# The first block products of a gMLP and MLP layer, taken row tile by row tile, with two sums moved to GpSimd

## What is computed

```python
def trunk(x):                                   # x: 1024 x 1024
    hn = rms_norm(x, norm1_g)
    u, v = split(gelu(hn @ a_w_in), 2)          # a_w_in: 1024 x 4096
    v = layer_norm(v) * a_ln_g
    sv = causal(a_ws) @ v + a_bs                # by chunks of 128 positions, 8 groups
    x = x + (u * sv) @ a_w_out                  # 2048 x 1024
    x = x + square(relu(rms_norm(x, norm2_g) @ mlp_w1)) @ mlp_w2
    return rms_norm(x, final_g)
```

## Time and profile before

| | us |
|---|---|
| median of 3 runs (1134.77 to 1135.09) | 1135.06 |
| the profiled execution, its own time | 1135.68 |
| its span in the trace | 1133.9 |
| PE busy | 1121.9 |
| DVE busy | 770.3 |
| ACT busy | 568.1 |
| POOL busy | 35.1 |

### The profile page before, as it was taken

One profiled execution on the slowest core, in us unless ns is written; L12 is line 12 of the kernel. 1 busy time (PEld: TensorE's weight loads), 2 busy tenths in 40 slices (PEclk: granted clock), 3 DMA queues, 4 the chain that ended last, 5 costly groups with the idle time before them and its releaser, 6 DMA issues.

```text
span 1133.9 us, 13195 instructions
## 1 busy us (share of the span) xinstructions
PE 1121.9 (99%) x5155; PEld 934.3 (82%) x5155; DVE 770.3 (68%) x832; ACT 568.1 (50%) x868; POOL 35.1 (3%) x22
## 2 busy tenths in 40 slices
PE   9999999999999999999999999999999999999997
PEld 8788888888888888888888888888888888888886
DVE  6986655578668986657667547456589575677666
ACT  8663434543554334656664464554653343433446
POOL 4000000000000000000000000000000000000240
PEclk9999999999999999999999999999999999999999
DMA  9054253262866494431343534527788254343213
GB/s 334 1 186 149 75 181 117 75 227 109 306 225 248 135 349 158 155 103 46 103 164 142 193 141 154 191 101 273 295 302 316 97 237 186 108 152 112 77 73 148
DMA packets 74765, 191.17 MB, mean 169 GB/s; under 512 B 3120, under 2 KB 4176, under 8 KB 68048
## 3 DMA queue, kind: packets, MB, share of 16 engines
q1 hardware_dynamic: 74496, 190.07, 46.4%
q10 hardware_dynamic: 208, 0.28, 0.1%
HBM read 131.61 MB, written 58.72 MB: 168 GB/s over the span
## 4 chain that ended last, share of the span: by engine, by line
PE 93%; ACT 2%; DVE 2%; issue 1%; DMA 1%; SPq 0%; DVEq 0%; ACTq 0%
PE banks L397 30%; PE banks L401 30%; PE banks L402 30%; PE banks L466 2%; DVE left_and_right L1289 1%; DMA rows<-in_x_dram 1%; PE banks L504 0%; ACT junk_b L1185 0%; ACT ring_high L894 0%; DVE ring_low L1253 0%; DVE raw_s L1358 0%; DVE rows L1433 0%; DVE scratch L1418 0%; ACT rows L1220 0%; ACT a_high L951 0%
## 5 line engine op out<-in xcount | busy, mean ns | idle before, releaser
L924 ACT ACTIVATE pair_high<-left_and_right 128x1024 fp32r<-128x1024 f32 x168 | 177.7, 1061 | 255.8 <-PE banks L397 208.1
L1253 DVE TENSOR_TENSOR ring_low<-left_and_right,ring_high 128x512 fp32r<-128x512 f32 x224 | 153.0, 691 | 213.1 <-ACT ring_high L894 212.7
L1261 DVE TENSOR_TENSOR pair_low<-left_and_right,pair_high 128x1024 fp32r<-128x1024 f32 x168 | 204.6, 1229 | 123.2 <-ACT pair_high L924 123.1
L894 ACT ACTIVATE ring_high<-left_and_right 128x512 fp32r<-128x512 f32 x224 | 139.4, 631 | 272.9 <-PE banks L397 175.9
L397 PE MATMUL banks<-pair_high 128*128 128x512 f32 x672 | 262.0, 390 | 0.1
L402 PE MATMUL banks<-pair_high,pair_low 128*128 128x512 f32 x672 | 261.5, 389 | 0.0
L401 PE MATMUL banks<-pair_low,pair_high 128*128 128x512 f32 x672 | 261.4, 389 | 0.0
L397 PE MATMUL banks<-s_high,ring_high 128*128 128x512 f32 x384 | 149.6, 389 | 0.0
L401 PE MATMUL banks<-s_low,ring_high 128*128 128x512 f32 x384 | 149.4, 389 | 0.0
L402 PE MATMUL banks<-s_high,ring_low 128*128 128x512 f32 x384 | 149.4, 389 | 0.0
L397 PEld LDWEIGHTS banks<-pair_high 128*128 128x128 f32 x672 | 126.1, 188 | 26.9 <-issue 0.4
(11 more groups left out here) (105 smaller groups left out, 1227.7 us busy)
## 6 DMA issues: line engine op xcount, KB each, us to landing
left_and_right<-sums SPq DMA_DIRECT2D x40, 1024.0 KB, 6.1
left_and_right<-in_mlp_w_dram SPq DMA_DIRECT2D x36, 1024.0 KB, 6.3
sums<-rows SPq DMA_DIRECT2D x34, 1024.0 KB, 5.1
left_and_right<-in_a_w_in_dram SPq DMA_DIRECT2D x19, 1024.0 KB, 6.2
v_blocks<-rows SPq DMA_DIRECT2D x8, 1024.0 KB, 4.5
left_and_right<-in_a_w_out_dram SPq DMA_DIRECT2D x8, 1024.0 KB, 10.3
spare<-v_blocks SPq DMA_DIRECT2D x6, 1024.0 KB, 5.8
sums<-spare SPq DMA_DIRECT2D x6, 1024.0 KB, 3.9
```

Source lines behind the costliest of these rows:

```text
L894: nc.scalar.activation(ring_high[k][:, :], right_place(n, pos)[:, k, :], ACT.Copy)\
L924: nc.scalar.activation(pair_high[pair_entry(d, pos, k)][:, :, :], pair_of(d, pos, k), ACT.Copy)\
L1253: nc.vector.tensor_tensor(ring_low[k][:, :], right_place(n, pos)[:, k, :], ring_high[k][:, :].bitcast(F32), ALU.subtract).then_inc(low_don ...
L1261: nc.vector.tensor_tensor(pair_low[e][:, :, :], pair_of(d, pos, k), pair_high[e][:, :, :].bitcast(F32), ALU.subtract).then_inc(low_done, 1)
```

## The change

1. The first product (A11) runs row tile by row tile. `first_turn(c)` turns the four k-tiles of row tile c into the one bank 4 + c, and `first_products(c, k)` makes the four units' share of that row tile. Row tiles 2 and 3, and A12, are turned between these products. The high and low part of A11 are now taken per row tile, and all ring places stay in use until row tile 3.
2. The gain is no longer per partition there, so DVE multiplies it in with the tile's scale: a row of `norm1_g` is loaded, spread over the partitions by a matmul with a row of ones (bank 3), and copied to `g1_b`.
3. A12's high and low part come straight from the banks. A21 and A22 are turned inside the second product by halves of 8 transposes, through the two banks 6 and 7.
4. S3 is made from the banks by k-tiles (`first_s3`, high part of A11 minus the gained A21) and completed by one sum with A11's low part (`first_s3_rest`); S2 and its split go by k-tiles. S4 takes two sums in place of one.
5. `raw_a11` isn't copied; POOL makes it again as high + low (`restore_a11`). The first weight sum moves from DVE to POOL (`first_sum_t`). Both stand ahead of the masking of `ws_nat` in POOL's list.
6. SP loads row tile 0, the first weight k-tile, row tile 1, the rest of that weight block, and then the other row tiles.

```diff
-            def first_turn():
-
+            def first_turn(c):
+
+                bank = 4 + c
+                begin_fill(("turn", 0, "a11"), bank)
+                pe.wait_ge(x_scaled, c + 1)
                 for k in range(4):
-                    begin_fill(("turn", 0, "a11"), 4 + k)
...
+            def first_block():
+
+                first_turn(0)
+                warm(FILL_A)
+                first_turn(1)
+                warm(FILL_B)
                 for c in range(4):
-                    pe.wait_ge(x_scaled, c + 1)
+                    first_products(c, 0)
+                    if c == 3:
+                        turn_half("a12", 1)
+                    first_products(c, 1)
+                    if c == 1:
+                        first_turn(2)
+                    if c == 2:
+                        turn_half("a12", 0)
+                    first_products(c, 2)
+                    first_products(c, 3)
+                    if c == 1:
+                        first_turn(3)
...
+            def next_block():
+
+                for m in range(4):
                     for k in range(4):
...
+                        next_products(m, k)
+                        if (m, k) in NEXT_TURNS:
+                            turn_half(*NEXT_TURNS[m, k])
...
             pe.wait_ge(ident_done, 1)
-            warm(3 * WARM_UP)
+            warm(2 * WARM_UP)
+            pe.wait_ge(g_row_landed, 16)
+            pe.wait_ge(ones_set, 1)
+            begin_fill("g_row", 3)
+            nc.tensor.matmul(ps[:, 3, :], one_row[:, :], g1_row, start=True, stop=True).then_inc(full[3], 1)
+            warm(2)
...
+            load_x(0)
             sp.dma_start(quarter[0][:, 0:1, :], weight(0, "b11")[:, 0:1, :]).then_inc(first_landed, 16)
+            load_x(1)
             load(("b11", 0), quarter[0][:, 1:4, :], weight(0, "b11")[:, 1:4, :], quarter_landed[0], "quarter0")
...
+            def first_s3(k):
...
+                nc.vector.scalar_tensor_tensor(out=raw_s3[:, k, :], in0=ps[:, bank, :], scalar=minus_g1[:, k:k + 1],
+                                               in1=high["a11"][:, k, :].bitcast(F32), op0=ALU.mult, op1=ALU.add)\
+                  .then_inc(drained[bank], 1)
...
                 if n == 0:
-                    low_combo(0, "a12")
-                    sum_t(0, 0)
-                    split_low(0, 1, 0)
-                    split_low(0, 1, 1)
-                    sum_combo(0, "s3")
-                    split_low(0, 1, 2)
-                    sum_combo(0, "s2")
-                    split_low(0, 1, 3)
+                    for k in range(4):
+                        first_s3(k)
+                    first_s3_rest()
+                    sum_t(0, 1)
+                    for k in range(4):
+                        first_s2(k)
...
+            def restore_a11():
+
+                for c in range(4):
+                    emptied(pool, ("turn", 0, "a11"), 4 + c)
+                nc.gpsimd.tensor_tensor(raw_a11[:, :, :], high["a11"][:, :, :].bitcast(F32),
+                                        low["a11"][:, :, :].bitcast(F32), ALU.add).then_inc(a11_restored, 1)
+
+            def first_sum_t():
+
+                q = {b: quarter[i][:, :, :] for b, i in places(0).items()}
+                pool.wait_ge(*landed["b12", 0])
+                pool.wait_ge(low_done, unit(0, 0, 3) + 1)
+                nc.gpsimd.tensor_tensor(q["b11"], q["b12"], q["b11"], ALU.subtract).then_inc(t_summed, 1)
...
             for m in range(MT - 2):
                 scale_x_b(m)
+            first_sum_t()
+            restore_a11()
             pool.wait_ge(ws_landed, 16)
```

385 lines of the change are left out of this document (262 added, 123 removed).

## The result

| | before | after |
|---|---|---|
| median, us | 1134.91 (5 runs, 1134.76 to 1135.09) | 1147.91 (5 runs, 1145.19 to 1149.40) |
| ratio, 95% interval | | 1.0112 [1.0102, 1.0123] |
| profiled execution, us | 1135.68 | 1149.40 |
| its span, us | 1133.9 | 1147.7 |
| S2's start, us | 43.24 | 56.98 |

What follows compares the result with a forecast made beforehand. PE bounds the kernel, but DVE decides S2's start: -1.1 (early start) + 3.5 + 3.3 (POOL holds) - 0.4 (turn waits) = +5.3 us on 1135.68, so 1141.0 profiled, 1140.4 as median; range 1132.5 to 1143.0.

Steps and rivals of the forecast that it cites:

- the landmark: Start of S2's product, the third, 43.24 us before: what it gains or loses, the whole kernel gains or loses.
- The start, 11.2: Kernel start: the first product matmul begins near 11.2 us, 2.6 us earlier than before.
- eight warm-ups: PE between the first two turns: 16 instructions, each like a transpose or slightly more, take 1.8 us.
- The holds, 3.5 and 3.3: DVE ahead of S2: POOL's two sums, 4.0 us each, hold `ring_low` 0 for 3.5 and the next `ring_low` for 3.3.
- PE's turn waits vanish in that (-0.4): DVE ahead of S2: its two waits for PE's half turns, 0.5 us, mostly disappear within the holds, saving 0.4.
- The 17.0 of the forecast: DVE's own instructions from `ring_low` 0 of the second product to S2, summed to 16.9 or 17.0 us.
- The sign for PE's last release: At S2's product, starting at 48.6: PE is released by `ring_low` and not by `s_low`.
- Case B: Ahead of S2: one POOL sum is hidden, about 0.9 us of its hold left; 1138.0 us, chance 0.18.
- Case C: Ahead of S2: POOL's sums cost nothing, leaving -1.1 us; 1134.0 us, chance 0.26.
- The gain of 1.1 us: At S2's start: new landmark 42.1 against 43.24, as long as POOL disturbs nobody.
- Case D: At S2: PE, not DVE, decides if DVE's list begins before 21 us; 1131.0 at best, 1132.5 for half, chance 0.16.
- the dear end of A: Ahead of S2: both POOL sums hold DVE, 1140.4 us, chance 0.40; with holds of 5.2 us each, 1142.8.

Runs made afterwards that it cites:

- e3: Changed kernel with the first T (weight) sum moved back to DVE, POOL keeping only the restoring of A11: 1147.44 us.
- e5: Changed kernel with each of POOL's two sums in four instructions of 512 elements in place of one of 2048: 1140.00 us, ratio 1.0041.
- e1: Changed kernel with both POOL sums (first weight sum, restoring of A11) given to DVE: 1141.99 us, ratio 1.0057.
- e9: e1 with sixteen identity products ahead of S2's product, one output block lost: 1141.52 us, in two groups, 1137.3 to 1137.8 and 1141.5 to 1141.8.
- e7: Changed kernel with 14 and 20 identity products behind the first two steps of the second product: 1150.21 us.
- e2: Changed kernel with the restoring of A11 moved back to DVE, POOL keeping only the first T (weight) sum: 1145.16 us.
- e10: Changed kernel's row-by-row start without POOL sums, weight sums and S2 in pieces, S1 as A21 + A22, late mask, part of output lost: 1136.40 us, ratio 1.0009.
- two small edits: Kernel before with POOL's mask waiting for the sixth product and S2's low part in four instructions, PE waiting for each k-tile: 1132.66 us, ratio 0.9981.
- e11: Kernel before with one wait added, so that POOL's mask of ws_nat waits for the sixth product's ring: 1134.36 us, ratio 0.9994.
- e4: Changed kernel with 16 warm-up identity products in place of 8 ahead of the spreading of the gain row: 1147.77 us.
- e6: Changed kernel with the gain row spread by a DMA in place of matmul and copy, and twelve warm-up products: 1147.10 us.
- e8: Kernel before with only the first T (weight) sum moved from DVE to POOL, ahead of the mask: 1137.08 us, ratio 1.0015.

## Why the prediction was right and wrong

The direction and the mechanism were right: DVE, not PE, bounds the stretch ahead of S2, POOL's two sums hold it, and the landmark carries the whole difference. The time was not: 1147.9 against a range up to 1143.0. The forecast put S2's start at 48.6; it is at 56.98, 8.4 us later. By its own steps:

- **The start, 11.2.** Measured 14.54 in the profiled execution. The order of the chain held, and the price of the spreading nearly (2.07 us against 1.7). The step that failed is PE's rate at the start, above all in "eight warm-ups (16 instructions, each like a transpose or slightly more, 1.8)". They took 3.37, which is 1.4 us of the miss by the distance to the next turn; 1.6 us more were lost ahead of row tile 0's turn, which began at 10.12 and not near 8.5, behind six identity instructions in 1.65 us that take 0.94 in e3. The rate was read from a kernel whose clock was up at 5.7 us, and this one's came up at 13.9. In other executions (e3, e5) 11.2 came true. Cost: 3.3 us, all of it handed on, since DVE's list began at 27.39, 3.3 us after the forecast's 24.1.
- **The holds, 3.5 and 3.3.** Measured 3.8 (4.52 less 0.69) and 5.1 (5.97 less the usual 0.9). The mis-sized term is the price of one POOL sum, taken as 4.0 "nearer the lower end": it is 4.55 and 4.97. The second sum met no `ring_low` but a scaling, which took 4.7 us, a hold of 4.3. The other 0.8 belong to a term that the forecast put at nothing: POOL's mask, now queued behind the sums, held the second scaling (1.3 in place of 0.5, the mask running from 36.24 for 1.28), as it did in e1. The forecast had read that hold in the kernel before, and counted it as gone without a reason. Cost: 0.3, 1.0 and 0.8, together 2.1 us. The figure that the prediction quoted beside it, 4497 ns for one POOL sum ("GPSIMD Engine Reference", section 3.1 of the Trainium skill), agrees with the first sum's 4.55 us.
- **"PE's turn waits vanish in that (-0.4)".** Of its 0.5 us that left 0.1; they became 0.79 + 2.11 = 2.9. This step took PE's rate as given. PE had fallen to 1.2 GHz in its first wait, and reached the half turns late: the waiting party made the waited-for party late in turn. Cost: 2.8 us.

These make 8.2 of the 8.4 us. That the loop closes through the clock is shown for the wait at S2 (e9). For the second product it rests on comparison: where the clock was whole between the two half turns of A21, DVE's wait for the second was 0.62 us (e1) and 0.85 (e7), and where it was at half for most of that time, 2.11 (changed kernel), 2.28 (e2) and 1.99 (e3).

- **The other terms held.** DVE's list from its first `ring_low` to S2's product took 29.6 us (27.39 to 56.98). The 17.0 of the forecast with the measured holds of 8.9 and turn waits of 2.9 make 28.8; 0.8 is left, for which the forecast had 0.4. The later landing of row tiles 2 and 3 made nobody wait, and S4's second sum shows no wait of PE behind S2. The sign for PE's last release held too: the trace names `s_low` for 56.98, but `s_low` ended at 56.28, and PE started when the first `ring_low` behind it, begun at 56.20, had had its 0.7 us.
- **Case B**, one hold hidden, is refuted: both showed in full, and each alone costs 3 us or more (e2, e3). What was to speak for it, that POOL waits as long as DVE leaves no gap, didn't happen here: `restore_a11` began at 31.32, while DVE finished its `ring_low`, and DVE's next instruction, begun at 31.84, stood until its end. It does happen in e10, where POOL's mask of 1.09 us takes 7.08, from 74.04 on, while DVE's instructions keep their usual lengths. **Case C** is refuted as well, and by more than POOL: even without the sums (e1) the time is 6.4 us over the kernel before, of which 2.2 is the weight sum on DVE. The gain of 1.1 us that cases A to C were built on needs the good start, a mask that holds nobody and a clock that doesn't fall; no run had all three with the weight sum off DVE, so the gain itself is neither shown nor refuted. **Case D** needed DVE's list to begin before 21 us; it began at 24.0 at best (e3).
- **The range** was built from the bounds of the holds only. The start and PE's rate entered as single numbers, so its upper end was the dear end of A. Both were also things that the rows of before couldn't price, since PE, once started, never stood still there for more than 1.05 us.

## What to carry to other kernels

When a change lets the bounding engine wait, price the wait twice: once for itself, and once for what PE's clock loses behind it (2.3 us for a wait of 3.5 us here, 1.65 for one of 2.57), and then ask who in turn waits for PE. Before giving GpSimd a long sum with SBUF inputs, look for a place where VectorE is idle or reads banks; failing that, cut it into pieces, which alone took about 7 of the 13 us back. And before rebuilding a start, look at the waits that PE really has: two small edits at the two of them gave 2.2 us, the rebuilt start none.

## What the runs showed of the hardware

- A sum of 2048 elements on GpSimd beside VectorE stops an instruction of VectorE with two SBUF inputs (4.52 us in place of 0.69), and one with a single SBUF input too (two scalings, 5.97 in place of 0.9). By the Trainium skill ("SBUF — State Buffer", section "Who interferes with whom") the latter holds for the forms that use both pairs of ports; the trace doesn't show which form ran. An instruction with one of its inputs in a PSUM bank wasn't held: two of `first_s3` took 1.40 us from 33.29 in e5, in the middle of POOL's pieces (29.42 to 35.76), and 1.40 in e1, where POOL was silent.
- At the end of a GpSimd sum VectorE got one turn and no more in the changed kernel: the next GpSimd sum was in place by 31.32, and VectorE's next instruction, begun at 31.84, ended only after it. In pieces (e5) VectorE got a turn after each. It can go the other way: in e10 GpSimd's mask stood for 7.08 us (1.09 in e11) while VectorE ran on with instructions of two SBUF inputs. What decides it is open.
- After 3.5 to 3.7 us without work PE's next matmul took 0.76 or 0.77 us in place of 0.47, at a granted clock of 0.50, in the changed kernel, e2, e4, e5 and e7, and in e1 behind S2. In e3 and e6, after 3.53 and 3.52 us, it took 0.47, and the clock fell only in the wait that followed. So the length of a wait alone doesn't decide. After 2.57 us in e8 the clock read 0.76 in the five microseconds around, and after 1.96 us in e1's second product 1.00 throughout. In the changed kernel it stayed at 0.50 from 31 to 44 us, while PE was busy for 6.4 us of these 13.
- At the start, identity products took 3.37 or 1.95 us for 16 instructions at the same place of the same list of instructions, while the granted clock read 1.00. That column counts the time ahead of the first clock record (13.9 us in the changed kernel, 6.1 in e3) as full, so near the start of a trace it is the durations that tell PE's rate.
